# One convolution unit in fp32 instead of four, attention heads with an empty piece behind every phase, and another turn of PSUM banks

## What is computed

```python
u = rmsnorm(h, g_mix)
proj = u @ w_in                       # 2048 x 10784
q, k, v, z, xbc, dt_raw, g_a, g_s = split(proj)
attn = sliding_window_sink_attention(rope(q), rope(k), v, sinks)   # 16 heads of 64
xbc = silu(causal_depthwise_conv(xbc, conv_w, conv_b))             # width 4, 3072 channels
dt = softplus(dt_raw + dt_bias)
y = ssd_chunked(xs, dt, -exp(a_log), bm, cm) + d_skip * xs
out = sigmoid(g_a) * (attn @ w_attn_br) + sigmoid(g_s) * (rmsnorm(y * silu(z)) @ w_ssd_br)
```

## Time and profile before

| | us |
|---|---|
| runs | 2746.88, 2745.01, 2747.53 (median 2746.88) |
| the profiled execution | 2745.93 |
| its span | 2744.1 |
| PE busy | 2705.7 (99%) |
| DVE busy | 1962.3 (72%) |
| ACT busy | 1413.3 (52%) |

### The profile page before, as it was taken

How to read it: one execution, slowest core, us unless ns; L and a number is a source line. 1 busy time by engine, 2 the same in 40 slices (tenths; PEclk the granted TensorE clock), 3 DMA queues, 4 the chain that set the end, 5 groups by cost and what they waited for, 6 DMA issues and landing times.

```text
span 2744.1 us, 41637 instructions
## 1 busy us (share of the span) xinstructions
PE 2705.7 (99%) x16606; PEld 2375.7 (87%) x16606; DVE 1962.3 (72%) x2948; ACT 1413.3 (52%) x2094; POOL 101.4 (4%) x189
## 2 busy tenths in 40 slices
PE   8999999999999999999999999999999999999998
PEld 7788888888888888888888889988888888888887
DVE  7568777757677776677666778887788775677765
ACT  6455556544455554455445552247665553455543
POOL 1320000000000000000000000000000000000000
PEclk9999999999999999999999999999999999999999
DMA  7466556655668878878656556864455556555554
GB/s 241 136 197 230 175 179 199 184 184 186 198 220 287 287 283 287 293 282 284 214 177 212 179 180 216 290 232 146 139 191 185 186 198 190 184 192 185 185 195 142
DMA packets 166611, 573.19 MB, mean 209 GB/s; under 512 B 19873, under 2 KB 26737, under 8 KB 165905
## 3 DMA queue, kind: packets, MB, share of 16 engines
q1 hardware_dynamic: 151216, 521.86, 57.5%
q0 software_dynamic: 15056, 48.65, 4.9%
q10 hardware_dynamic: 144, 0.01, 0.0%
HBM read 530.86 MB, written 38.90 MB: 208 GB/s over the span
## 4 chain that ended last, share of the span: by engine, by line
PE 91%; DVE 5%; ACT 2%; DMA 1%; issue 1%; POOL 0%; DVEq 0%; SPq 0%; ACTq 0%; POOLq 0%
PE PS L951 91%; DVE wl L1914 1%; DVE CC L1922 1%; DMA raw<-in_w_in 1%; ACT wh L1372 0%; PE PS L1287 0%; DVE SQA L1914 0%; DMA XC<-KTC 0%; DVE QT L1914 0%; ACT SX1b L1372 0%; DVE H L1914 0%; DMA RO<-QT 0%; ACT AHt L1372 0%; DMA H<-in_xT 0%; DVE Z L1914 0%
## 5 line engine op out<-in xcount | busy, mean ns | idle before, releaser
L1914 DVE TENSOR_TENSOR wl<-raw,wh 128x1024 fp32r<-128x1024 f32 (+3 forms) x892 | 1044.5, 1195 | 463.0 <-ACT wh L1372 461.1
L1372 ACT ACTIVATE wh<-raw 128x1024 fp32r<-128x1024 f32 (+3 forms) x892 | 899.1, 1032 | 520.9 <-PE PS L951 415.0
L951 PE MATMUL PS<-CHt,wh 128*128 128x512 f32 x2816 | 885.9, 395 | 0.0
L951 PE MATMUL PS<-BIGt,wh 128*128 128x512 f32 (+1 forms) x2816 | 754.8, 356 | 3.2 <-DVE wl L1914 1.4
L951 PE MATMUL PS<-AHt,wh 128*128 128x512 f32 (+1 forms) x2080 | 635.9, 386 | 14.6 <-DVE wl L1914 11.5
L951 PEld LDWEIGHTS PS<-CHt,wl 128*128 128x128 f32 x2816 | 529.0, 188 | 124.9
L951 PE MATMUL PS<-CHt,wl 128*128 128x256 f32 x2816 | 553.5, 278 | 0.0
L951 PEld LDWEIGHTS PS<-BIGt,wl 128*128 128x128 f32 x2304 | 434.7, 189 | 79.0 <-issue 0.2
L951 PE MATMUL PS<-BIGt,wl 128*128 128x256 f32 x2304 | 497.7, 279 | 0.0
L951 PEld LDWEIGHTS PS<-BIGt,wh 128*128 128x128 f32 x2816 | 433.6, 190 | 8.1 <-issue 5.1
L951 PEld LDWEIGHTS PS<-AHt,wl 128*128 128x128 f32 x1952 | 367.9, 188 | 79.8 <-issue 0.7
(11 more groups left out here) (311 smaller groups left out, 1623.4 us busy)
## 6 DMA issues: line engine op xcount, KB each, us to landing
raw<-in_w_up SPq DMA_DIRECT2D x264, 512.0 KB, 5.0
raw<-in_w_in SPq DMA_DIRECT2D x200, 512.0 KB, 4.3
raw<-in_w_down SPq DMA_DIRECT2D x132, 512.0 KB, 4.3
raw<-in_w_gate SPq DMA_DIRECT2D x88, 512.0 KB, 5.3
raw<-in_w_down SPq DMA_DIRECT2D x56, 384.0 KB, 3.5
raw<-in_w_ssd_br SPq DMA_DIRECT2D x32, 512.0 KB, 4.3
raw<-in_w_o SPq DMA_DIRECT2D x32, 512.0 KB, 4.4
PKR<-in_w_in SPq DMA_DIRECT2D x32, 512.0 KB, 5.2
```

The source lines that it names most:

```text
L951: return e.matmul(o, l, r, start=start, stop=stop, skip_group_check=True)
L1372: return e.activation(o, x, f, **k)
L1914: return e.tensor_tensor(o, x, y, op)
```

## The change

1. `FULL_XBC` holds unit 0 alone, so units 2, 4 and 6 (twelve slices) are split and multiplied in three passes, and evacuated by a join.
2. A head gets an empty step behind each of its four phases instead of behind phases 1 and 2. The first head's first phase still stands behind slice 26, the last head's last one behind slice 62 (before: 55), and `cums` behind 65 and 66 (before: 57 and 58).
3. The series of `dt` stands in five phases behind phase 0, so behind slices 31 to 35, instead of all behind slice 31; three stages may be live in lane conv instead of two.
4. The layer norm of the mixer has 15 phases. Its products on PE move from phase 4 to 5 and from 7 to 8, what follows them moves by one.
5. `pieces`: the units `pp2` and `pp6` of the per-layer projection skip a bank; a unit of one bank now avoids both banks of a unit of two ahead of it, and `ca0` goes to the counter's second place. In the mixer the banks so run 0, 1, 2 instead of 2, 0, 1, and in the last units of the mixer the two banks of a pair, and of the units ahead, change places.

```diff
-FULL_XBC = (0, 2, 4, 6)
+FULL_XBC = (0,)
...
-LN_END = 14
-LN_BANK = (0, 4, 7)
+LN_END = 15
+LN_BANK = (0, 5, 8)
...
 def attn1_stage(t, late):
-    return stage("attn1", t, 4, late, (1, 2))
+    return stage("attn1", t, 4, late, (0, 1, 2, 3))
...
         add("w_in", 0, 16, 3584 + 256 * i, "U1", "ev_xbc", i, mode="full" if i in FULL_XBC else "turn",
-            gens2=([2] if i == 0 else []) + [stage("conv4", i, 5)] + ([stage("dt", 0, 2)] if i == 0 else [1] if i == 11 else []))
+            gens2=([3] if i == 0 else []) + [stage("conv4", i, 5)] + ([stage("dt", 0, 6)] if i == 0 else [1] if i == 11 else []))
...
-        if u.mode in ("one", "parked") and n and not aside and u.banks[gb % len(u.banks)] == us[n - 1].bank:
+        if u.ev == "ev_pp" and u.i in (2, 6):
+            gb += 1
+        front = () if n == 0 else us[n - 1].pair if us[n - 1].bank is None else (us[n - 1].bank,)
+        while u.mode in ("one", "parked") and (
+                u.banks[gb % len(u.banks)] in front or u.ev == "ev_ca" and u.i == 0 and gb % 3 != 1):
             gb += 1
...
-            elif ph == 4:
-                after_odd(4)
+            elif ph == 5:
+                after_odd(5)
...
-            e.wait_ge(st, 8)
-            ts(w_, q_, 1.0 / 17, 1.0 / 15, MUL, ADD).then_inc(st)
-            for j, c in enumerate((13, 11, 9, 7, 5, 3, 1)):
+            if ph == 2:
+                e.wait_ge(st, 8)
+                ts(w_, q_, 1.0 / 17, 1.0 / 15, MUL, ADD).then_inc(st)
+            for j in {2: (0, 1), 3: (2, 3), 4: (4, 5), 5: (6,)}.get(ph, ()):
                 e.wait_ge(st, 9 + 2 * j)
                 tt(w_, w_, q_, MUL).then_inc(st)
```

More of the change, by code:

```diff
@@ L749, in hybrid_block_kernel @@
              "trc": (a2_a[1], "ptc"), "tr1": (a2_a[1], "pt1")}
-    LN_READ = {0: "mean", 4: "rs", 7: "sp"}
+    LN_READ = {0: "mean", 5: "rs", 8: "sp"}
     def sync_program(e):
@@ L1259, in ln @@
                 tok.then_inc(ln_pe.sem)
-            elif ph == 7:
-                after_odd(7)
+            elif ph == 8:
+                after_odd(8)
                 e.wait_ge(ln_d.sem, ln_d.at(0, "rec"))
@@ L1807, in ln @@
                     af(LNB[c // 2][:, c % 2, :], CC[c][:, :], ACT.Square).then_inc(ln_a.sem)
-            elif ph == 5:
+            elif ph == 6:
                 e.wait_ge(ln_d.sem, ln_d.at(0, "rs"))
                 af(RS2, RS2, ACT.Sqrt).then_inc(ln_a.sem)
-            elif ph in (9, 10):
-                for c in range(4 * ph - 36, 4 * ph - 32):
+            elif ph in (10, 11):
+                for c in range(4 * ph - 40, 4 * ph - 36):
                     e.wait_ge(ln_d.sem, ln_d.at(0, f"v{c}"))
                     af(LNB[c // 2][:, c % 2, :], CC[c][:, :], ACT.Tanh).then_inc(ln_a.sem)
-            elif ph in (11, 12):
-                for c in range(4 * ph - 44, 4 * ph - 40):
+            elif ph in (12, 13):
+                for c in range(4 * ph - 48, 4 * ph - 44):
                     e.wait_ge(ln_d.sem, ln_d.at(0, f"z{c}"))
@@ L2088, in dt @@
                 return
[L2089 to L2096, removed]
-            e.wait_ge(st, 8)
-            ts(w_, q_, 1.0 / 17, 1.0 / 15, MUL, ADD).then_inc(st)
-            for j, c in enumerate((13, 11, 9, 7, 5, 3, 1)):
+            if ph == 1:
+                e.wait_ge(dt_a.sem, 1)
+                ts(s_, e_, 2.0, None, ADD).then_inc(st)
+                e.wait_ge(st, 5)
+                e.reciprocal(s_, s_).then_inc(st)
+                e.wait_ge(st, 6)
+                tt(s_, s_, e_, MUL).then_inc(st)
+                e.wait_ge(st, 7)
+                tt(q_, s_, s_, MUL).then_inc(st)
+            if ph == 2:
+                e.wait_ge(st, 8)
+                ts(w_, q_, 1.0 / 17, 1.0 / 15, MUL, ADD).then_inc(st)
+            for j in {2: (0, 1), 3: (2, 3), 4: (4, 5), 5: (6,)}.get(ph, ()):
                 e.wait_ge(st, 9 + 2 * j)
@@ L2102, in dt @@
                 e.wait_ge(st, 10 + 2 * j)
[L2103 to L2110, removed]
+                ts(w_, w_, 1.0 / (13, 11, 9, 7, 5, 3, 1)[j], None, ADD).then_inc(st)
+            if ph == 5:
+                e.wait_ge(st, 23)
+                tt(w_, w_, s_, MUL).then_inc(st)
+                ts(x, x, 0.0, None, MAX).then_inc(st)
+                e.wait_ge(st, 25)
+                stt(x, w_, 2.0, x, MUL, ADD).then_inc(st)
+                e.wait_ge(st, 26)
+                stt(AN, x, -1.0, two(alog), MUL, MUL).then_inc(st)
         def cums(_, ph):
@@ L2494, in ln @@
                 tt(SQA[:, 0, :], SQA[:, 0, :], SQA[:, 1, :], ADD).then_inc(st)
-            elif ph == 4:
+            elif ph == 5:
                 e.wait_ge(ln_pe.sem, ln_pe.at(0, "q"))
                 ts(rs, PS[:, 7, 0:2], 1.0 / 1024, 1e-6, MUL, ADD).then_inc(st)
-            elif ph == 6:
+            elif ph == 7:
                 e.wait_ge(ln_a.sem, ln_a.at(0, "root"))
                 e.reciprocal(rs, rs).then_inc(st)
-            elif ph == 7:
+            elif ph == 8:
                 e.wait_ge(ln_pe.sem, ln_pe.at(0, "sp"))
@@ L2506, in ln @@
                     tt(CC[c][:, :], CC[c][:, :], mean, MUL).then_inc(st)
-            elif ph == 8:
+            elif ph == 9:
                 e.wait_ge(hg_d.sem, 1)
@@ L2511, in ln @@
                     ts(CC[c][:, :], CC[c][:, :], vec("lng", c), vec("lnb", c), MUL, ADD).then_inc(st)
-            elif ph in (10, 11):
-                for c in range(4 * ph - 40, 4 * ph - 36):
+            elif ph in (11, 12):
+                for c in range(4 * ph - 44, 4 * ph - 40):
                     e.wait_ge(ln_a.sem, ln_a.at(0, f"t{c}"))
                     stt(CC[c][:, :], LNB[c // 2][:, c % 2, :], 1.0, CC[c][:, :], ADD, MUL).then_inc(st)
-            elif ph in (12, 13):
-                for c in range(4 * ph - 48, 4 * ph - 44):
+            elif ph in (13, 14):
+                for c in range(4 * ph - 52, 4 * ph - 48):
                     low(x, c, CC[c][:, :], 1.0)
```

## The result

The changed kernel takes 2767.52 us (median of 6 runs, 2767.07 to 2768.22), the kernel before 2746.34 in the same series: ratio 1.0078, interval 1.0068 to 1.0088, so 21.2 us slower. The span of the profiled execution grew from 2744.1 to 2765.3 us.

A forecast was written before the change was run, and what follows sets the result against it. DVE's in-order list, with its waits for ACT, was taken to pace PE, itself busy 99%: 2745.93 + 17.7 - 1.0 = 2762.6, against the median 2763.6, given as 2763 us; range 2744 to 2770.

The forecast's parts named there:

- the stretch: Convolution slices with attention work, up to slice 78: forecast to begin at 287.8 us instead of 270.07, +17.7 us.
- DVE's list: DVE's in-order work from slice 32's low half to the last head's reciprocal: 109.3 + 92.4 + 31.8 + 2.2 = 235.7 us.
- closed blocks: DVE's waits for ACT's high half behind score groups and reciprocals: six more of 2.8 and six of 2.5, 31.8 us.
- B: Rival: in the convolution stretch only the first three gates hurt, 10.8 us, then DVE catches up; 2746 us; chance 0.14.
- C: Rival: DVE has slack in the convolution stretch, PE sets the pace, the kernel gets faster; 2735 us; chance 0.12.
- D: Rival: the clock stays down over several slices, or a bank in the mixer blocks; over 2770 us; chance 0.04.
- The gates: PE's waits for slice 33's low half and before the transposes of heads 1 to 7: 27.3 us together.
- the clock behind the last gate: PE's lower granted clock after the last long wait in the convolution stretch: 0 to 1.7 us, none taken.
- PE's gain: Twelve convolution slices in three passes: 12 x 0.76 = 9.1 us, less 1.6 for slices behind attention work, so 7.5.
- The term -1.0: Net for the mixer's layer norm and the banks: -1.0 us, bounds -2.9 to +1.5.
- The banks: New turn of banks: removes the first gate unit's 1.23 wait, little remains; two late-read banks cost 0.1 and 0.2 us.
- The spread: Empty piece behind all phases of the heads: moves work and makes none, its price already in DVE's list.

The follow-up runs named there:

- Run 5: Changed kernel, with the split put ahead of phases 0 and 1 of the first heads in ACT's list alone; 2743.48 us, ratio 0.9988.
- run 1: Kernel before with only FULL_XBC cut to unit 0; heads, dt series, layer norm and banks as before; 2776.97 us, ratio 1.0108.
- run 12: Changed kernel with the split ahead in ACT's list, layer norm in 14 phases, and heads' gaps behind phases 1 and 2 alone; 2740.59 us, ratio 0.9981.
- Run 8: Kernel before with the new turn of banks and the split ahead of the first heads' phases 0 and 1 in ACT's list; 2745.73 us, ratio 0.9993.
- Run 6: Changed kernel with the layer norm back in 14 phases; splits, spread and banks kept; 2767.18 us, ratio 1.0071.
- run 9: Kernel before with FULL_XBC cut to unit 0 and the new turn of banks; heads, dt and norm as before; 2765.35 us, ratio 1.0067.
- run 10: Kernel before with only empty pieces behind all phases of the heads and the new turn of banks; 2763.97 us, ratio 1.0065.
- run 2: Changed kernel with FULL_XBC back at units 0, 2, 4, 6; spread heads, dt phases, layer norm and banks kept; 2757.92 us, ratio 1.0039.
- run 3: Changed kernel, phases 0 and 1 of the first heads put behind their slice's first split on DVE and ACT; 2761.70 us, ratio 1.0052.

## Why the prediction was right

The forecast was 2763 us and slower, by +17.7 in the stretch and -1.0 behind it; measured were 21.2 more, 18.8 to slice 78 and 2.4 behind. The mechanism is the one that was forecast; two terms of the sum, 4.5 us together, were off.

**DVE's list.** It was summed to 235.7 us for the last head's reciprocal and 237.1 for its scaling; the reciprocal ended at 235.1 and the transposes began at 236.67. The twelve closed blocks stand in the trace of the changed kernel one by one: six of 2.77 to 2.79 behind score groups and six of 2.50 to 2.51 behind reciprocals up to there, with a first wait of 1.97 where 2.2 was put. Together they are 31.7 us, where 31.8 was put. That the whole sum came out so close has some luck in it: three more waits for the high half, 1.7 us together (0.24, 0.94 and 0.51), weren't in the list, and the work with its small gaps took 90.8 instead of 92.4. Run 5 shows the blocks to be the cause. Rivals B and C are out: waits are found to the end, and with the blocks DVE has no slack. D's bank that blocks in the mixer is found in run 1, but not in the changed kernel. B's and C's idea, that PE then sets the pace, is what run 5 and run 12 show once the blocks are open.

**The gates**, PE's waits for the low half of slice 33 and at the heads. Forecast were 0.8, 4.1, 5.9, 3.3, 2.6, 4.9, 2.0, 3.7, in sum 27.3; measured were 0.82, 3.80, 3.95, 1.07, 2.62, 3.40 (2.85 at head 4's values and 0.55 at head 5's transposes), 2.81, 2.31, in sum 20.8. The places are right, the sum isn't, because the slices between them ran slower: the granted clock is 0.93 in the window in which PE is busy 115.00 us. That was said (each wait is followed by slower slices, and the next wait shrinks by as much). An estimate of the size: over the stretch PE is busy 180.78 us, and it was 179.96 before, although 7.5 us of work were to go, so some 8 us went to the clock, all but 1.5 of them ahead of the last gate. By that gate the difference cancels, as its time shows (236.67, forecast 237.1).

**What was too small: the clock behind the last gate.** The prediction allowed 0 to 1.7 us for it and took none. From the last head's transposes to slice 78 it has 50.7 us (237.1 to 287.8), measured were 52.2 (236.67 to 288.91). In the first four microseconds, 236.67 to 240.67, the granted clock is 0.62, from 245 to 289 it is 1.00. These 1.5 us, less the 0.4 by which the gate came early, are the difference between +17.7 and +18.8.

**PE's gain.** Forecast 9.1 - 1.6 = 7.5. Run 8, without waits, has a stretch of 179.00 with four fp32 units; run 12 has 176.49 with one, less its wait of 3.70 is 172.8: 6.2 less, an estimate, at a granted clock of 0.99 where run 8 has 1.00. The two also differ in dt's phases.

**What was wrong: the mixer.** The term -1.0 (bounds -2.9 to +1.5) came out at +2.4. The step that failed priced the norm's second product alone. That gave about what was said (1.64 fell to 0.20, and 0.25 came behind it, 1.2 us together); but the norm's tanh on ACT moved by a piece too and stands ahead of the transposes' copies, and the waits there grew by 3.5 us. Run 6 shows those waits to be the norm's. Their net is 2.3 us by the waits, and 1.0 between the traces of run 6 and the changed kernel, because the clock fell in run 6 and not in the other; why it falls behind the same wait in one execution and not in the next isn't settled. The banks were put at about nothing: right against the kernel before, where their wait of 1.23 went and others came, for a net of 0.3 in the traces; wrong as a judgement of that part, since without it the splits would have met the wait of 10.64 us.

**What was incomplete: the spread.** It was said to move work and make none. Beside the splits that holds: with them the heads may be spread or not (stretch 201.58, and 200.33 in run 9). But alone it costs 16.6 us, with dt in phases 9.5. The two costs do not add up. The likely reason, which no run tests by itself, is that either of them makes DVE the pace-maker, and then the other has nothing left to take. For run 10's wait of 6.13 the cause stands in its rows; for the 2.4 to 2.6 that PE waits in runs 2 and 10 for a low half near 150 us the cause is open.

**Readings of the prediction that were off.** The window from 72 to 80 us, given for the clock, holds only the last 1.4 us of the wait of 3.2, which began at 70.2. And its two windows do not differ in their busiest engine: PE leads in both (93.92 of 96.30 and 61.50 of 61.50 us); what changes is DVE's share, from 64% to 86%. Neither enters the sum.

## What to carry to other kernels

Where two engines run their lists in order and hand work to each other, read idle time as blocks with a place, not as a share that can be filled: an engine that was busy 93.78 of 135.80 us, 69%, set the pace here, because each of its waits was closed by the other engine's next instruction. Give each engine its own order at such a place: the same instructions, with ACT's copy one step earlier, were worth 24 us in the changed kernel, and next to nothing in the kernel before (run 8), where the blocks did not set the pace. And when the number of units with two banks changes, follow the bank counter to the end of the program. The Trainium skill, page "Perfetto Trace Analysis", section "Optimization Strategy", says to find what blocks the engine in its gaps and make that start sooner or end faster; runs 3 and 5 agree, and show that it matters on which engine's list that is done (5.3 against 24.2 us).

## What the runs showed that was not expected

The spread of the heads costs 16.6 us alone and 9.5 with dt in phases (runs 10 and 2), the splits 18.0 to 19.7 (runs 9 and 1); together they gave 19.2 us. A shift of the bank counter more than 1,300 us ahead of its effect cost 10.64 us at one place. And a wait of DVE taken off one instruction came back at another in nearly full size (2.78 at the low half, 2.37 at the join), as long as ACT's order stayed as it was.
